# The modulation vectors of two adaLN layers, made one at a time in four groups of 32 array columns

## The reference, cut to what matters

```python
cmod = jax.nn.silu(c)                                   # 9 x 1024 in all
for l in range(DEPTH):                                  # DEPTH = 2
    mod = cmod @ p['w_ada'][l] + p['b_ada'][l]          # 1024 x 6144 weights per layer
    sh1, sc1, g1, sh2, sc2, g2 = [u[:, None, :] for u in jnp.split(mod, 6, axis=-1)]
    h = rmsnorm(x, p['norm_g'][l, 0]) * (1 + sc1) + sh1
    ...                                                 # layer 0: HGRN2 mixer, 8 heads; layer 1: mLSTM
    x = x + g1 * mix
    h = rmsnorm(x, p['norm_g'][l, 1]) * (1 + sc2) + sh2
    x = x + g2 * hier_moe(h, ...)
```

## Time and profile before

| | |
|---|---|
| median of 3 runs | 2647.31 us (2647.21 to 2649.17) |
| the profiled execution, span of its instructions | 2648.1 us |
| PE busy | 2473.5 us, 93% of the span |
| PEld / DVE / ACT / POOL busy | 63% / 30% / 17% / 5% |
| chain that ended last | PE 83%, DVE 7%, DMA 4% |
| modulation matmuls (L437) | 384 records, 169.2 us busy |
| mean granted TensorE clock | 0.942 of full speed |

### The profile page before, as it was taken

How to read it: one execution, slowest core, us unless ns; L and a number is a source line. 1 busy time by engine, 2 the same in 40 slices (tenths; PEclk the granted TensorE clock), 3 DMA queues, 4 the chain that set the end, 5 groups by cost and what they waited for, 6 DMA issues and landing times.

```text
span 2648.1 us, 26856 instructions
## 1 busy us (share of the span) xinstructions
PE 2473.5 (93%) x10008; PEld 1669.8 (63%) x10009; DVE 782.2 (30%) x1701; ACT 442.5 (17%) x674; POOL 120.0 (5%) x193
## 2 busy tenths in 40 slices
PE   8999999999699999989979999999999988999996
PEld 1487878347477788666753654736537755877765
DVE  0134344211511111244563443433432033111112
ACT  0223233210310000121121220312201030000001
POOL 0000000000100000000002011020010010000000
PEclk9999999979779999989989999999999995999998
DMA  9412121651014444221116224062242110344420
GB/s 358 174 58 73 64 73 65 216 190 64 0 48 159 159 162 162 72 83 37 51 43 221 81 98 180 24 229 73 82 165 84 64 40 0 135 159 158 159 88 37
DMA packets 77782, 290.67 MB, mean 110 GB/s; under 512 B 8912, under 2 KB 8912, under 8 KB 76928
## 3 DMA queue, kind: packets, MB, share of 16 engines
q1 hardware_dynamic: 54432, 200.57, 21.9%
q0 software_dynamic: 23264, 88.88, 9.3%
HBM read 241.94 MB, written 47.48 MB: 109 GB/s over the span
## 4 chain that ended last, share of the span: by engine, by line
PE 83%; DVE 7%; DMA 4%; ACT 3%; issue 2%; DVEq 0%; ACTq 0%; POOL 0%; SPq 0%; POOLq 0%
PE ps L409 21%; PE ps L659 15%; PE ps L668 8%; PE ps L437 6%; PE ps L627 4%; PE ps L489 3%; PE ps L865 3%; PE ps L685 3%; PE ps L421 3%; DMA arena<-in_c 2%; PE ps L874 2%; PE ps L858 2%; DMA out_mc_s<-arena 2%; PE ps L837 2%; PE ps L454 2%
## 5 line engine op out<-in xcount | busy, mean ns | idle before, releaser
L409 PE MATMUL ps<-hT,ring 128*128 128x288 f32 x1792 | 452.5, 413 | 14.9 <-ACT hT L939 11.5
L409 PEld LDWEIGHTS ps<-hT,ring 128*128 128x128 f32 x1792 | 343.7, 193 | 112.9 <-issue 12.2
L659 PE MATMUL ps<-arena,ring 128*128 x2048 | 399.4, 356 | 0.0
L659 PEld LDWEIGHTS ps<-arena,ring 128*128 128x128 f32 x2048 | 386.8, 190 | 10.4 <-issue 8.9
L668 PE MATMUL ps<-ring,arena 128*128 128x512 f32 (+1 forms) x512 | 221.0, 592 | 0.0
L409 PE MATMUL ps<-arena,ring 128*128 128x288 f32 x768 | 191.4, 413 | 3.7 <-DVE arena L1808 3.7
L409 PEld LDWEIGHTS ps<-arena,ring 128*128 128x128 f32 x768 | 148.6, 194 | 46.1 <-DVE arena L1808 4.2
L437 PE MATMUL ps<-ring,cols 128*9 128x512 f32 x384 | 169.2, 603 | 8.7 <-DMA ring<-in_wstream 8.1
L668 PEld LDWEIGHTS ps<-ring,arena 128*128 128x128 f32 (+1 forms) x512 | 90.3, 176 | 125.3 <-issue 125.3
L858 PE MATMUL ps<-arena 128*64 128x512 f32 x256 | 123.4, 612 | 17.8 <-DMA arena<-in_c 17.0
L1506 DVE TENSOR_TENSOR arena<-ps,arena 128x224 f32<-128x224 f32 x64 | 25.1, 392 | 359.0 <-PE ps L659 359.0
(11 more groups left out here) (372 smaller groups left out, 2334.1 us busy)
## 6 DMA issues: line engine op xcount, KB each, us to landing
ring<-in_wstream SPq DMA_DIRECT2D x376, 512.0 KB, 3.3
arena<-in_c POOLq DMA_DIRECT2D x64, 512.0 KB, 4.7
out_mc_s<-arena POOLq DMA_DIRECT2D x64, 512.0 KB, 4.0
arena<-in_hg POOLq DMA_DIRECT2D x8, 512.0 KB, 3.9
out_hg_s<-arena POOLq DMA_DIRECT2D x8, 512.0 KB, 2.9
out_mc_p<-arena POOLq DMA_DIRECT2D x16, 256.0 KB, 2.4
xT<-in_xT SPq DMA_DIRECT2D x1, 2304.0 KB, 16.7
x_dram<-xT POOLq DMA_DIRECT2D x1, 2304.0 KB, 9.1
```

Of the source, the lines that this page charges most:

```text
L409: mm = pe.matmul(ps[:, 2 * p + half, 0:TH], ring[:, r, c * P:(c + 1) * P], rhs(k)[:, TH * half:TH * (half + 1)], start=(k == 0), stop=(k = ...
L659: mm = pe.matmul(ps[:, 2 * p, 0:W], ring[:, r, c * P:(c + 1) * P], mo["hs"][:, c, bass.ds(at_g, W)], start=(c == 0), stop=(c == DC - 1))
```

## The change

The twelve vectors (two layers of six, 1024 columns each) are made one at a time. A vector takes eight slots, which SP now loads in another order, so that two neighbouring slots hold the same two input blocks for both halves of the vector's columns. For each input block, four matmuls follow each other: group g has the 32-column stationary operand (nine rows and zeros), 256 of the vector's 1024 columns as the moving operand, and PSUM partitions 32g to 32g+31 of bank 0 as its output. ACT copies 128 x 256 to SBUF, two 128 x 128 transposes turn it, and DVE adds the bias in four small operations and frees the pair of banks.

Two vectors stand before the first norm. One stands in each of the eight heads, between `values` and `scan` (its transposes after `scan`). The last two stand after the last head's `values` and `scan(6)`, and after `scan(7)`. The scale factors of the later norms are made after the heads. SP's loads down to wo are written out one by one.

```diff
+ORDER, _ = laid([("ada_first", 2 * DC), ("hg", H * N_PER_HEAD), ("ada_last", 2 * DC)] + AFTER)
...
+            load_vector(0)
             sp.dma_start(xT, io["xT"]).then_inc(x_in, 16)
-            with sp.Fori(1, NSLOT // R) as i:
+            load_vector(1)
+            for h in range(H):
+                for q in range(4):
+                    load(ORDER["hg"] + N_PER_HEAD * h + q, SLOTS["hg"] + 4 * h + q)
+                load_vector(h + 2)
...
-            def ada_rows(layer):
...
-                            for kk in range(2):
-                                mm = pe.matmul(ps[0:NV, 2 * p, :], silc[:, 2 * si + kk, :],
-                                               ring[:, r, kk * 512:(kk + 1) * 512],
...
+            def ada_rows(turn, at, freed):
+
+                pe.wait_ge(pair_free[0].sem, freed)
+                for q in range(0, DC, 2):
+                    rs = [(at + q + half) % R for half in range(2)]
+                    for half in range(2):
+                        pe.wait_ge(slot_full[rs[half]], 16 * (turn + ((at % R + q + half) // R + 1)))
+                    for kk in range(2):
+                        for g in range(4):
+                            col_at = 512 * kk + 256 * (g % 2)
+                            mm = pe.matmul(ps[32 * g:32 * (g + 1), 0, 0:256], silc[:, q + kk, :],
+                                           ring[:, rs[g // 2], col_at:col_at + 256],
+                                           start=(q + kk == 0), stop=(q + kk == DC - 1))
+                            if kk and g % 2:
+                                used.on(mm)
+            def turn_ada_rows(u, freed):
+
+                pe.wait_ge(pair_free[0].sem, freed + 1)
+                pe.wait_ge(pair_free[1].sem, freed)
+                for b in range(2):
+                    mm = pe.transpose(ps[:, 2, P * b:P * (b + 1)], modrow[:, u, P * b:P * (b + 1)], ident)
+                s["turned"].on(mm)
...
+            ada_rows(0, 0, 1)
+            turn_ada_rows(0, 1)
+            ada_rows(1, R, 2)
             norm_sums(0)
-            turn_ada_rows(0)
+            turn_ada_rows(1, 2)
...
                     project(1 - u, i + u)
                     scores(u, i)
                     values(1 - u, i + u)
+                    head_ada(1 - u, i + u)
                     scan(u, i)
+                    head_turned(1 - u, i + u)
...
             scan(0, last)
-            ada_rows(1)
+            head_turned(1, last)
+            ul, al = USES["ada_last"] // 2, ORDER["ada_last"]
+            ada_rows(al // R, al, ul)
             scores(1, last)
             scan(1, last)
-            pe.wait_ge(s["s_ready"].sem, 4 * H)
-            turn_ada_rows(1)
+            turn_ada_rows(0, ul)
+            ada_rows((al + DC) // R, al + DC, ul + 1)
+            turn_ada_rows(1, ul + 1)
...
+            ada_rows(0, ada_slot(NA - 2) + DC)
             exponentials(H - 1)
-            ada_rows(1)
             head_norm(H - 1)
+            ada_rows(1, ada_slot(NA - 1) + DC)
...
+            def modulation(n):
+
+                dve.wait_ge(s["turned"].sem, n + 1)
...
+                for g in range(4):
+                    ins = tt(dst[:, g], src[:, g], bias[:, g].unsqueeze(2).broadcast_to([P, 2, NV]), ALU.add)
+                pair_free[1].on(ins)
...
+            modulation(2)
             with looped(dve, H // 2, per) as i:
                 for u in range(2):
                     elementwise(u, 2 * i + u)
                     scan(u, i)
-            modulation(1)
+                    modulation(2 * i + (u + 3))
+            modulation(NA - 1)
```

More of the change, by code:

```diff
@@ L65, with laid @@
 N_XM, N_Z, N_MD = MT, MT, DC * MT // 8
[L66 to L72, removed]
+def laid(parts):
+    at, out = 0, {}
+    for name, n in parts:
+        out[name] = at
+        at += n
+    return out, at
+AFTER = [("wo", N_WO), ("moe0", G * N_GROUP), ("xm", N_XM), ("z", N_Z), ("md", N_MD), ("moe1", G * N_GROUP)]
+SLOTS, NSLOT = laid([("ada0", N_ADA), ("hg", N_HG), ("ada1", N_ADA)] + AFTER)
+NA = LAYERS * 6
+N_PER_HEAD = 4 + DC
+ORDER, _ = laid([("ada_first", 2 * DC), ("hg", H * N_PER_HEAD), ("ada_last", 2 * DC)] + AFTER)
+assert all(SLOTS[name] == ORDER[name] for name, _ in AFTER)
 USES = {}
@@ L80, with ada_slot @@
     _at += _n
+def ada_slot(n):
+    if n < 2:
+        return ORDER["ada_first"] + DC * n
+    if n < NA - 2:
+        return ORDER["hg"] + N_PER_HEAD * (n - 2) + 4
+    return ORDER["ada_last"] + DC * (n - NA + 2)
 def offsets(spec):
@@ L184, in build @@
             ("keep", T)])
-        modrow = [carve([("rows", 6 * D)], start)[0]["rows"] for start in (0, hg_end)]
+        ada, ada_end = carve([("silc", DC, 32), ("rows", 2, 256)], hg_end)
+        silc, modrow = ada["silc"], ada["rows"]
+        assert ada_end <= 24000
+        mod_of = modt.rearrange("p l j n -> p (l j) n").rearrange("p (u g b) n -> p u g b n", u=NA, g=4)
         mo, _ = carve([
@@ L286, in _, with load, load_vector @@
             sp.dma_start(cols[:, :], io["cols"]).then_inc(small_in, 16)
-            for r in range(R):
-                sp.dma_start(ring[:, r, :], wstream[r]).then_inc(slot_full[r], 16)
-            sp.dma_start(xT, io["xT"]).then_inc(x_in, 16)
-            with sp.Fori(1, NSLOT // R) as i:
+            def load(at, src):
+                if at >= R:
+                    sp.wait_ge(s["slot_used"].sem, at + 1 - R)
+                sp.dma_start(ring[:, at % R, :], wstream[src]).then_inc(slot_full[at % R], 16)
+            def load_vector(n):
+                src = SLOTS[f"ada{n // 6}"] + DC * (n % 6)
+                for q in range(DC):
+                    load(ada_slot(n) + q, src + 4 * (q % 2) + q // 2)
+            load_vector(0)
+            sp.dma_start(xT, io["xT"]).then_inc(x_in, 16)
+            load_vector(1)
[3 more added lines that the diff above has]
+                load_vector(h + 2)
+            for n in range(NA - 2, NA):
+                load_vector(n)
+            with sp.Fori(ORDER["wo"] // R, NSLOT // R) as i:
                 for r in range(R):
@@ L940, in norm, with ada_rows @@
                                                        bias=modt[:, n // 2, 24 * (n % 2) + c, 0:1]))
[L942 to L948, removed]
+            def ada_rows(u, done):
+                act.wait_ge(used, done)
+                pair_free[0].on(act.copy(modrow[:, u, :], ps[:, 0, 0:256]))
             for p in range(2):
@@ L954, in _ @@
             act.wait_ge(small_in, 16)
-            s["silc"].on(act.activation(silc, silc, ACT.Silu))
-            ada_rows(0)
+            act.wait_ge(s["silc_clear"].sem, 1)
+            s["silc"].on(act.activation(silc[:, :, 0:NV], col("c", DC, NV), ACT.Silu))
+            for n in range(2):
+                ada_rows(n, ada_slot(n) + DC)
             act.wait_ge(x_in, 16)
@@ L1213, in by_seq, with scales @@
                 return ap.rearrange("p (b t) -> p b t", b=NB)
[L1215 to L1221, removed]
+            def modulation(n):
+                dve.wait_ge(s["turned"].sem, n + 1)
+                src = ps[:, 2, 0:256].rearrange("p (b g n) -> p g b n", b=2, g=4)[:, :, :, 0:NV]
+                bias = col("bada", NA, 4, 2)
+                if isinstance(n, int):
+                    dst, bias = mod_of[:, n], bias[:, n]
+                else:
+                    dst = mod_of[:, bass.ds(n, 1)].rearrange("p u g b n -> p (u g) b n")
+                    bias = bias[:, bass.ds(n, 1)].rearrange("p u g b -> p (u g) b")
+                ins = None
+                for g in range(4):
+                    ins = tt(dst[:, g], src[:, g], bias[:, g].unsqueeze(2).broadcast_to([P, 2, NV]), ALU.add)
+                pair_free[1].on(ins)
+            def scales(layer, k):
+                g = col("ng", LAYERS, 2, DC)[:, layer, k, :].unsqueeze(2).broadcast_to([P, DC, NV])
+                V.link(dve, stt(amod[:, layer, k], modt[:, layer, 24 * k + 8:24 * k + 16, :], 1.0, g, ALU.add, ALU.mult))
             def norm(n):
@@ L1254, in _ @@
             s["yg_ready"].base = 1
+            s["silc_clear"].on(dve.memset(silc, 0.0))
             dve.wait_ge(small_in, 16)
-            modulation(0)
+            for n in range(2):
+                modulation(n)
+            dve.wait_ge(pair_free[1].sem, 3)
+            scales(0, 0)
             norm(0)
```

67 lines of the change are left out of this document (32 added, 35 removed).

## The result

The changed kernel takes 2566.37 us (median of 4 runs, 2560.63 to 2568.76) against 2647.87 for the kernel before beside it: a ratio of 0.969, 95% interval 0.9677 to 0.9704, some 81 us less. The profiled execution has a span of 2563.1 us.

What follows compares the result with a forecast made beforehand. The prediction took PE (TensorE), busy for 93% of the span, as the bound. Its terms, -57.1 + 72.1 - 64.6 + 6.4 = -43.2 us, took the median 2647.3 to 2604 us, range 2562 to 2672.

Steps and rivals of the forecast that it cites:

- the first rival: Vector matmuls: all four column groups run abreast, 4.0 us a vector, 2570 us in total; chance 0.27.
- the case that I held likeliest: Vector matmuls: neighbouring groups overlap only by one record, 7.7 us a vector, 2604 us in total; chance 0.43.
- x: Time of one vector's matmuls on PE: put at 7.7 us, with 4.0 and 13.8 as the ends.
- The third rival: Vector matmuls: one after another with loads in the open, 19.5 us a vector, 2735 us in total; chance 0.12.
- A: Start, up to the first projection: two vectors bound by transfers, first projection at 53.7 instead of 110.8, -57.1 us.
- B: Heads: eight vectors with their transposes, tile-form switches and delays added, +72.1 us.
- the delay of the evict: Heads: DVE's four additions delay the next `elementwise`, and ACT's evict behind it, 0.9 us each time, 6.3 in all.
- C: Gap before the last scores: 21.2 us after the scan instead of 85.8, -64.6 us, PE idle for some 12.
- D: Last head and tail: scores at the low clock +2.5 us, last vector before the output projection +3.9, together +6.4.
- The rest: The later 2054 us of the kernel: untouched, same loads in the same order, no change.
- Four abreast: The first rival: four column groups at work together, 4.0 us a vector, 2570 us in total; chance 0.27.
- One after another: Second rival, vector matmuls: the groups' records don't overlap, 13.8 us a vector, 2668 us in total; chance 0.18.

Runs made afterwards that it cites:

- e2_grouped: The change with each pair of slots' matmuls issued group by group instead of alternating the groups: 2566.9 us.
- e4_norm_first: The change with the first norm's squares, sums and root moved ahead of the second vector: 2559.9 us.
- e5_in_scan: The change with each head's vector inside the scan, behind its output matmuls and ahead of PE's wait for ACT's squares: 2558.7 us.
- e7_two_groups: The change with two column groups of 512 columns instead of four of 256: 2589.1 us.
- e1_serial: The change with every vector's matmuls in one column group, two of 512 columns per input block, one after another: 2664.0 us.
- e0_after: The changed kernel itself, unaltered, run and profiled again: 2566.6 us.
- e8_decay_first: e6_all with ACT doing the last head's exponentials ahead of the copy of vector 10: 2539.4 us.
- e6_all: The change with vector inside the scan, first norm's sums before second vector, additions in DVE's head-norm wait, and POOL's states loaded later: 2545.4 us.

## Why the prediction was right and where it was wrong

The direction was right; the likeliest time, 2604, was 38 us too slow. The measured one lies in the stated range (2562 to 2672) because the range took in the first rival, to which I gave 0.27; it lies outside the 2592 to 2622 of the case that I held likeliest. So the range held by its width, not by the mechanism that I chose.

**x failed.** The step was: "the two records of one float32 matmul go to the same group, so the second waits for the first, and what follows in the queue waits behind it". The second does wait for the first, but what follows does not wait behind it: four groups start within 20 ns, and each goes on at its own record's pace (e2_grouped). x is 3.66 us, and 4.7 with the slots' wait, not 7.7. In the rows of before one matmul follows another on the same columns throughout, so the order of the queue and the order within a group could not be told apart there; I let the queue decide. Even the rival's 4.0, put between 3.4 and the 4.6 of 64 pairs of load and matmul at 0.072 us, was slightly high; pairs here take 3.66 / 64 = 0.057.

The Trainium skill ("TensorE: Matmul & The Clock Gate", Part 3, The mechanism and the speedups behind it) has matmuls in different positions of the array start some 4 ns apart; between column groups one sees 7 here. It also has matmuls start and end in program order, which e2_grouped contradicts for the starts. It lists loads as overlapping matmuls only where the rows differ, though The mechanism also lets a load into the background weight buffer go ahead. Here 64 loads of all 128 rows are hidden in the vector's 3.66 us, so the list's rule does not hold as it stands. The third rival fell with that.

**A held** (-57.6 against -57.1), since it is a term of the transfers: slots come in pairs some 2.6 us apart, a pair's matmuls take a quarter of x, so x does not show in it. The second vector's slots come at 26 to 36 us, POOL's states among them, and the sums start at 38.6. e4_norm_first shows what the term left standing: 10 us that needed no vector.

**B was mis-sized, by x for the most part.** 8 vectors at 7.7 in place of 4.7 (x with slots) make 24 of the 28.5 us between +72.1 and +43.6. Smaller parts: the delay of the evict, put at 6.3, raised PE's wait from 3.4 to 3.9, and moving the additions away is worth 1.8 to 2.7; the slots' wait, nothing at my x and 0.3 a head at x = 4, is 0.8; the transposes, put at 2 us for eight heads, are busy for 4.6; and the head norm's sums take 13.0 instead of 8.7 us, which I did not foresee. They ran at 606 ns a record, behind a vector and a wait; with the wait covered they ran at 432 (e5_in_scan). The difference is the granted clock, here during the sums of one head, in the change and in e7_two_groups:

```profile
303.76:306.05 2.29, 2.29 (x5) 1.61 (x6) 0.00 (x0) 1.25 (x1) 0.00 (x0) 0.50 1.03 408
266.85:268.09 1.24, 1.24 (x6) 0.98 (x7) 0.00 (x0) 1.24 (x1) 0.00 (x0) 1.00 1.00 406
```

Neither the wait nor the narrow matmuls lower it by themselves: the kernel before, e1_serial and e7_two_groups all have the same wait of 0.8 us ahead of the sums, the latter two behind a vector of 32-column matmuls in the same place, and run them at 432. What sets the change apart from e7_two_groups is the vector in four groups, shorter and with a wait for slots inside it; which of these does it, no run here separates. Nor is all of it time added to the stage, whose mean granted clock is 0.96 before and after (0.95 in e0_after).

**C held** within 2 us: the idle time of PE is 14.4 us, released by DVE as said, and e8_decay_first with e6_all shows the bound to be DVE's chain or, where vector 10 is late, ACT's copy ahead of it.

**D** came out at -1.2: the last head +0.6 (+2.5 was put; the scores alone went from 4.18 to 7.04 us, but the granted clock now rises before the head ends, 0.81 from 505 to 510 us, where it was 0.50 from 582 to 594), the tail up to the projection +1.1 (+6.9, at x = 4 +3.2), the projection's start -2.9 (-3). The projection's part held. In the tail the vector takes 4.72 us, 1.1 more than the 3.66 of e5_in_scan, so the 3 us put for the low clock were too many.

**The rest** was put at nothing and, without the projection's start, shows -3.3. The spread of the same stage over ten profiles is 11.6 us, and the one profile of before, 2.9 us taken off (2051.2), lies in it; I count it to no part of the change.

**The rivals.** Four abreast (2570) is what happened, 4 us from the median. One after another (2668) is e1_serial's 2664, so its sum was right too. The 10.6 us for each us of x were loosely summed: the four terms as written give 8 in B, 1 each in C and D and 0.25 in A, 10.25. That a change of order alone would lose was the main risk, and the sign rested on x.

## What to carry to other kernels

A matmul with a few stationary columns and many moving ones can be cut into four column groups of 32, and on this chip the four ran abreast (3.66 us against 13.92 in one group); what is worth checking first is whether an ordering change alone pays (here it lost 0.7%). Work that is made short enough goes where PE waits for another engine, here behind the scan's output, and it must not stand, on any engine, ahead of the chain that PE waits for next. Where a wait was hidden by the long version of a stage, cost it in the open before shortening that stage.

## What the runs showed of the hardware beyond that

- Column groups do not wait for one another's place in the program: records of four groups start in sets of four every 0.216 us whether the program alternates the groups or not. 64 float32 records of 256 columns in four groups take 3.66 us, 32 of 512 in two groups 7.06, 32 in one group 13.92.
- Two 128 x 128 transposes behind the head norm's sums took 386 ns a record in the change and 276 ns in e5_in_scan, the sums 606 and 432: the same instructions, at a granted clock of 0.50 to 1.00 in the one and 1.00 in the other. Behind vectors in one group or two, with the same wait, they ran at 277 and 276, the sums at 432.
